# Unread products at the program borders, a reordered odd mixer and later rank products

## The reference

```python
x = x + (0.5 * (1.0 + mod[:, 2]) * f1).astype(x.dtype)
h = _adaln(x, w['norm_gain'][l, 1], mod, 1)
# even layer: gated DeltaNet heads | RWKV-7 heads;  odd layer: GLA heads | mLSTM heads
x = x + ((1.0 + mod[:, 5]) * o).astype(x.dtype)
```

```python
# C: qd = q*exp(bc); att = causal(qd @ (k*exp(-bc))); kd = k*exp(bc_last - bc)
#    o = att @ v + qd @ S;  S = S*exp(bc_last) + kd^T @ v
# D: dm = exp(log_d - m_t) * (q @ k^T); num = w_in*(q @ C) + dm @ v; den likewise
#    h = num / max(|den|, exp(-m_t)); then an RMS norm and a gate for both
```

```python
w_raw = w['w0_b'][i] + jnp.tanh(w_lr) @ w['w_w2'][i]
a = jax.nn.sigmoid(w['a0_b'][i] + a_lr @ w['w_a2'][i])
```

## Time and profile before

| | us |
|---|---|
| median of 3 runs | 2659.85 |
| the profiled execution | 2658.36 |
| its span, first to last instruction | 2656.6 |
| TensorE busy | 2541.6 |
| VectorE busy | 1604.7 |
| ScalarE busy | 1057.3 |
| POOL busy | 650.2 |

### The profile page before, as it was taken

How to read it: one execution, slowest core, us unless ns; L and a number is a source line. 1 busy time by engine, 2 the same in 40 slices (tenths; PEclk the granted TensorE clock), 3 DMA queues, 4 the chain that set the end, 5 groups by cost and what they waited for, 6 DMA issues and landing times. The chain is left out here.

```text
span 2656.6 us, 52472 instructions
## 1 busy us (share of the span) xinstructions
PE 2541.6 (96%) x22720; PEld 2389.8 (90%) x22720; DVE 1604.7 (60%) x2302; ACT 1057.3 (40%) x1546; POOL 650.2 (24%) x499
## 2 busy tenths in 40 slices
PE   6999999999999899999999999999999679999998
PEld 4999999888787787999999999999989569999998
DVE  5678726665465555677842677852743356677825
ACT  4444414554344322444432544432432333444513
POOL 0455201000010031155501055500100312355301
PEclk8999999999999979999999999999999789999999
DMA  6332455631000014222255322255751213222324
GB/s 238 104 120 95 157 192 193 236 131 54 29 3 3 9 60 163 64 95 93 93 194 177 121 90 96 96 183 175 234 200 60 76 52 105 66 94 96 101 83 133
DMA packets 82846, 303.30 MB, mean 114 GB/s; under 512 B 9376, under 2 KB 17072, under 8 KB 81336
## 3 DMA queue, kind: packets, MB, share of 16 engines
q1 hardware_dynamic: 82616, 299.95, 34.2%
HBM read 289.16 MB, written 10.76 MB: 113 GB/s over the span
## 5 line engine op out<-in xcount | busy, mean ns | idle before, releaser
L175 DVE TENSOR_TENSOR weights_r<-work,weights_r 128x1024 fp32r<-128x1024 f32 (+2 forms) x309 | 389.6, 1261 | 339.2 <-ACT weights_r L171 339.2
L171 ACT ACTIVATE weights_r<-work 128x1024 fp32r<-128x1024 f32 (+2 forms) x309 | 299.1, 968 | 534.0 <-PE banks L1498 298.9
L1379 POOL TENSOR_TENSOR rows<-rows,consts 128x288 f32<-128x288 f32 (+3 forms) x64 | 82.1, 1282 | 711.8 <-ACT consts L1641 711.8
L1496 PE MATMUL banks<-low_r,weights_r 128*128 128x288 f32 (+1 forms) x1064 | 255.3, 299 | 0.0
L1397 PE MATMUL banks<-big_r,weights_r 128*128 128x288 f32 x768 | 227.0, 296 | 0.0
L1398 PE MATMUL banks<-h_r,weights_r 128*128 128x288 f32 x768 | 226.6, 295 | 0.0
L1396 PE MATMUL banks<-h_r,weights_r 128*128 128x288 f32 x768 | 226.5, 295 | 0.0
L1494 PE MATMUL banks<-h_r,weights_r 128*128 128x288 f32 (+1 forms) x808 | 201.7, 307 | 4.7 <-DVE big_r L437 4.7
L1496 PE MATMUL banks<-big_r,weights_r 128*128 128x288 f32 (+2 forms) x800 | 202.0, 298 | 0.0
L175 DVE TENSOR_TENSOR ring_r<-consts,ring_r 128x1024 fp32r<-128x1024 f32 (+1 forms) x87 | 105.7, 1215 | 153.1 <-ACT ring_r L171 153.1
L1498 PE MATMUL banks<-h_r,weights_r 128*128 128x288 f32 (+1 forms) x808 | 195.3, 299 | 0.0
(11 more groups left out here) (581 smaller groups left out, 7084.9 us busy)
## 6 DMA issues: line engine op xcount, KB each, us to landing
work<-w_ff_dram SPq DMA_DIRECT2D x117, 512.0 KB, 3.6
h<-w_mod_dram SPq DMA_DIRECT2D x48, 768.0 KB, 5.3
consts<-w_ff_dram SPq DMA_DIRECT2D x59, 512.0 KB, 3.6
work<-w_down_dram SPq DMA_DIRECT2D x55, 512.0 KB, 3.5
big_buf<-w_mod_dram SPq DMA_DIRECT2D x24, 768.0 KB, 6.1
consts<-w_down_dram SPq DMA_DIRECT2D x33, 512.0 KB, 3.5
work<-w_down_dram SPq DMA_DIRECT2D x33, 384.0 KB, 3.4
work<-w_mod_first_dram SPq DMA_DIRECT2D x24, 512.0 KB, 12.0
```

The source lines that it names most:

```text
L171: return act.activation(high, raw, ACT.Copy)
L175: return engine.tensor_tensor(low, raw, high.bitcast(F32), ALU.subtract)
L1379: pool.tensor_tensor(k.rows[:, c], k.rows[:, c], k.square[:, c], ALU.add).then_inc(added, 1)
L1496: pe.matmul(out[a], high[:, w], x[a][1], start=False, stop=False)
```

## The change

1. `unread` issues products of two constant 128 x 128 matrices into a bank that nothing reads: 8 or 10 ahead of the first unit of each `dense_chain`; 10 at the end of the chain with the even projection (behind a wait for `unit7` of VectorE), 12 at the end of the one with the odd projection (behind `cols` of ScalarE); 8 in `even_prompt` ahead of `sq1_0` of chunk 0.
2. The rank product `r` goes from ahead of step 4 to ahead of step 6 of its piece (L1474).
3. In `odd_mixer`: the logs of the chunks are issued without waits, each with its semaphore. POOL masks the logs of chunk c between te and Kl of the same chunk, not one chunk ahead. TensorE does weights(0) ahead of front(1). ScalarE starts with Vc and Vd of chunk 0, and does Lexp and xw of i+2 right behind exponents(i+2), ahead of KL(i+1) and the root. VectorE does weights(1) behind front(1).

```diff
+def unread(k, pe, bank, count):
+    for _ in range(count):
+        pe.matmul(bank[:, 0:P], k.mask("ident"), k.mask("ones"), start=True, stop=True)
...
+                    if u is units[0]:
+                        unread(k, pe, banks(u, u.pieces[0])[:, 0], 8 if begin else 10)
...
-                            if even_gates and kt == KT // 2 and i in range(even_at(20), even_at(24)):
+                            if even_gates and kt == KT - 2 and i in range(even_at(20), even_at(24)):
                                 even_gates.rank(pe, "r", i - even_at(20))
...
+                if even_gates:
+                    pe.wait_ge(*even_gates.q.after("dve", "unit7"))
+                    unread(k, pe, k.psum[6], 10)
+                if odd_gates:
+                    pe.wait_ge(*odd_gates.q.after("act", "cols"))
+                    unread(k, pe, k.psum[6], 12)
...
+                        if c == 0 and g == G[0]:
+                            claim(f"sq1_{g}", c)
+                            unread(k, pe, two_banks(f"sq1_{g}", c)[0:P, 0], 8)
...
-        act += square_act(c) + of(i + 2, front_act) + of(i + 1, lambda b: at(b, ["KL"])) + at(c, ["root"]) \
-            + of(i + 2, weight_act)
+        act += square_act(c) + of(i + 2, front_act) + of(i + 2, log_act) + of(i + 1, lambda b: at(b, ["KL"])) \
+            + at(c, ["root"]) + of(i + 2, value_act)
...
-                    sp.wait_ge(logs_in, 16 * c)
                     chunk_logs(c)
...
-                pool.wait_ge(constants.landed, 32)
-                masked_logs(ODD_ORDER[0])
                 for i in places:
                     c = ODD_ORDER[i]
-                    if i + 1 < len(ODD_ORDER):
-                        masked_logs(ODD_ORDER[i + 1])
                     if c != SAMPLE:
                         relative(c, i)
                     to_the_end(c, i)
+                    masked_logs(c)
                     keys_to_end(c, i)
...
                 front(ODD_ORDER[0])
+                weights(ODD_ORDER[0])
                 front(ODD_ORDER[1])
-                weights(ODD_ORDER[0])
...
+                evict(ODD_ORDER[0], 0)
                 exponents(ODD_ORDER[0], 0)
-                evict(ODD_ORDER[0], 0)
+                log_exponents(ODD_ORDER[0], 0)
+                exponents(ODD_ORDER[1], 1)
+                keys(ODD_ORDER[0], 0)
+                log_exponents(ODD_ORDER[1], 1)
                 evict(ODD_ORDER[1], 1)
-                keys(ODD_ORDER[0], 0)
-                exponents(ODD_ORDER[1], 1)
```

More of the change, by code:

```diff
@@ L3409, in odd_orders @@
     front_act = lambda c: pick(c, "X Xn xl F", "X Xn xl")
-    weight_act = lambda c: at(c, ["Vc", "Vd"] + [f"Lexp_{h}" for h in range(2 if c == SAMPLE else 4)] + ["xw"])
+    log_act = lambda c: at(c, [f"Lexp_{h}" for h in range(2 if c == SAMPLE else 4)] + ["xw"])
+    value_act = lambda c: at(c, ["Vc", "Vd"])
     square_act = lambda c: pick(c, "sqC_0 sqC_1 sqD_0 sqD_1", "sqC sqD")
@@ L3419, in odd_orders @@
     of = lambda i, names: names(ODD_ORDER[i]) if i < len(ODD_ORDER) else []
-    masks_pool = lambda i: of(i, lambda c: at(c, ["lm"]))
-    pe = of(0, front_pe) + of(1, front_pe) + of(0, weight_pe)
-    act = of(0, front_act) + of(0, weight_act) + of(1, weight_act) + at(ODD_ORDER[0], ["KL"]) + of(1, front_act)
-    dve = of(0, front_dve) + of(0, weight_dve) + of(1, weight_dve) + of(0, masked_dve) + of(1, front_dve)
-    pool = masks_pool(0)
+    pe = of(0, front_pe) + of(0, weight_pe) + of(1, front_pe)
+    act = of(0, value_act) + of(0, front_act) + of(0, log_act) + of(1, front_act) + at(ODD_ORDER[0], ["KL"]) \
+        + of(1, log_act) + of(1, value_act)
+    dve = of(0, front_dve) + of(0, weight_dve) + of(0, masked_dve) + of(1, front_dve) + of(1, weight_dve)
+    pool = []
     for i in places:
         c = ODD_ORDER[i]
-        pool += masks_pool(i + 1)
         if c != SAMPLE:
@@ L3431, in odd_orders @@
         pe += of_sample(i + 1, "sc0 sc1") + (out_pe(SAMPLE) if of_sample(i + 1, "co") else [])
-        act += square_act(c) + of(i + 2, front_act) + of(i + 1, lambda b: at(b, ["KL"])) + at(c, ["root"]) \
-            + of(i + 2, weight_act)
+        act += square_act(c) + of(i + 2, front_act) + of(i + 2, log_act) + of(i + 1, lambda b: at(b, ["KL"])) \
+            + at(c, ["root"]) + of(i + 2, value_act)
         dve += sums_dve(c) + of(i + 1, masked_dve) + scaled_dve(c) + of(i + 2, front_dve) + of(i + 2, weight_dve)
         dve += of_sample(i, "SC2 SC3 SD2 SD3 SD4 SD5") + gated_dve(c) + of_sample(i + 1, "SC0 SC1 SD0 SD1")
-        pool += pick(c, "rel te Kl eC eD", "te Kl eC eD KEm KLm")
+        pool += pick(c, "rel te lm Kl eC eD", "te lm Kl eC eD KEm KLm")
     return pe, act, dve, pool
@@ L3492, in odd_mixer @@
         states_in, cleared, n_ready = (ph.sem(x) for x in ("states_in", "cleared", "n_ready"))
-        logs_in, sample_logs_in, entries_in = (ph.sem(x) for x in ("logs_in", "sample_logs_in", "entries_in"))
+        sample_logs_in, entries_in = (ph.sem(x) for x in ("sample_logs_in", "entries_in"))
+        logs_in = [ph.sem(f"logs_in_{c}") for c in range(NCH)]
         log_of = lambda c: log_rows[:, c * 4 * n:(c + 1) * 4 * n].rearrange("p (h i) -> p h i", h=4)
@@ L3513, in chunk_logs @@
                 def chunk_logs(c):
-                    sp.dma_start(log_of(c), log[None, :, c * n:(c + 1) * n].to_broadcast([P, 4, n])).then_inc(logs_in, 16)
+                    sp.dma_start(log_of(c), log[None, :, c * n:(c + 1) * n].to_broadcast([P, 4, n])).then_inc(logs_in[c], 16)
                 chunk_logs(0)
@@ L3601, in masked_logs @@
                         pool.wait_ge(sample_logs_in, 32)
+                        pool.wait_ge(constants.landed, 32)
                         tt(v2(log_rows_s), v2(log_rows_s), k.half("cut_below8")[:, None, :].to_broadcast([P, 2, m]), ALU.add)\
@@ L3604, in masked_logs @@
                         return
-                    pool.wait_ge(logs_in, 16 * (c + 1))
+                    pool.wait_ge(logs_in[c], 16)
+                    pool.wait_ge(constants.landed, 32)
                     tt(log_of(c), log_of(c), k.big("cut_below")[:, None, :].to_broadcast([P, 4, n]), ALU.add)\
@@ L3856, in evict @@
                 def evict(c, i):
-                    w = size(c)
                     act.wait_ge(*after("pe", "vct", c))
@@ L3864, in evict, with log_exponents @@
                         .then_inc(*did("Vd", c))
+                def log_exponents(c, i):
+                    w = size(c)
                     act.wait_ge(*after("pool", "lm", c))
@@ L3906, in _ @@
                         exponents(ODD_ORDER[i + 2], i + 2)
+                        log_exponents(ODD_ORDER[i + 2], i + 2)
                     if i + 1 < len(ODD_ORDER):
@@ L4066, in _ @@
                 weights(ODD_ORDER[0], 0)
-                weights(ODD_ORDER[1], 1)
                 masked(ODD_ORDER[0], 0)
                 front(ODD_ORDER[1], 1)
+                weights(ODD_ORDER[1], 1)
                 for i in places:
```

## The result

The changed kernel took 2634.66 us (median of 4 executions, 2631.5 to 2636.6) beside 2656.4 for the kernel before (4, 2651.05 to 2662.24): a ratio of 0.9921, 95% interval 0.9899 to 0.9943. A second comparison of the same two kernels gave 2639.76 against 2658.66, ratio 0.9931 (0.9910 to 0.9951). So 19 to 22 us were won by the medians (18 to 21 by the ratios), where 10.6 were forecast. The executions of one kernel lie up to 18 us apart here (26 of the kernel before: 2643.95 to 2661.5), so the intervals are some 0.2% to either side.

A forecast was written before the change was run, and what follows sets the result against it. TensorE was taken to set the end nearly everywhere, so only its waits or low clock pay. Terms -4.3 - 8.6 + 1.9 + 0.4 + 0 = -10.6 took 2658.36 to 2647.8, median 2649; range 2640 to 2657.

The forecast's parts named there:

- Later rank products: Even projection: TensorE's four waits of 1.07 us ahead of r vanish, gain 4.3 us.
- rival (c): Even projection: the rank wait only moves to the next w, total 2653 us; chance 0.08.
- Start of the odd mixer: Odd mixer's start: outputs of chunk 0 begin at 2095.2, 8.6 us earlier; ends 5.4 and 11.
- Everything starts about 0.75 us later: Odd mixer's start: the 12 unread products ahead of it delay everything by about 0.75 us.
- Steady rounds: Odd mixer's rounds: moved table load, Lexp and xw make round 1's root 1.9 us later; ends 0 and 5.7.
- The price of an unread product: Chain ends and borders: 0.11 us each at the odd border, 0.24 at half clock ahead of sq1_0.
- Round 0 still has the exponentials' table, and klt ends behind Lexp: nothing: Odd mixer, round 0: ScalarE's new order changes its time by nothing.
- a full clock gives at most some tenths: Ahead of the two output projections: first unit bound by VectorE's splits, so unread products gain only tenths; term 0.
- rival (d): Odd mixer's samples' part falls to half clock, at most 16 us more, 2665 us; chance 0.09.
- (b): Odd mixer: start gives only 5.4 through late logs, or ScalarE binds three rounds; 2653 us; chance 0.19.
- Rival (a): Clock kept over borders: -2.1 for +0.4 in the even mixer, -2 at the start; 2644.5 us; chance 0.12.
- rival (e): Everywhere: unread products don't hold the clock; already in the sum, no separate chance.

The follow-up runs named there:

- e2: Kernel before with only the reordered odd mixer, no unread products or later ranks: 2647.99 us, ratio 0.9960.
- j1: h3 plus 12 unread products in every odd mixer round, between the two groups' transposes: 2630.84 us, ratio 0.9907 to the kernel before.
- i1: Kernel before, old order, plus 22 unread products ahead of the odd mixer's first key transposes and 7 behind its second front: 2653.47 us, ratio 0.9978.
- e4: Changed kernel without its unread products (later ranks and reordered odd mixer kept): 2639.12 us, ratio 0.9941 to the kernel before.
- h2: Kernel before, old order, plus 20 unread products behind the odd mixer's first front, queued behind the waiting key transposes: 2660.95 us, ratio 1.0007.
- e3: Kernel before with only the six groups of unread products added: 2656.81 us, ratio 1.0003.
- h3: Changed kernel with ScalarE's old steady order, unread products only at dense 2 and 3 (10 each) and the odd start's wait (24): 2634.03 us, 0.9921 to before.

## Why the prediction was wrong

The direction was right, and the terms for the ranks, the start and the steady rounds were near. The size was half, since the sum had no term for the clock of untouched work.

- **Later rank products**, forecast -4.3: -4.6 in every trace with them. The wait did not move to the next `w`, rival (c) is out.
- **Start of the odd mixer**, forecast -8.6: -7.9 up to the first outputs in this pair of profiles, -6.1 against the second profile of before, and -7.2 between the averages (four profiles with the old start and nothing added there, two of the changed kernel). It is near, with a wrong part in it. "Everything starts about 0.75 us later" was 2.0: the next program's first work came 2.0 us behind the last projection product before (2078.45) and 4.0 after (2068.18). Only 1.0 of that reached the outputs: in e2, without the unread products, they come 18.5 us behind that product, not 19.5.
- **Steady rounds**, forecast +1.9: +1.4 to +2.3, 1.6 on average, around the root of round 1 in the nine profiles with ScalarE's new order, and 0.0 to +0.8, 0.4 on average, in the eight others (j1 aside). So the order costs some 1.2: the right mechanism, the size somewhat less.
- **The price of an unread product** was mis-sized. I took 0.11 us, from four transposes in 0.60. But a transpose is one instruction and a product of two such matrices is two: 24 instructions in 2.84 us, so 0.24 at full clock, and 4.05 for ten where the first 3.3 us go at half clock. All 58 are 116 instructions, and keep TensorE busy for 20.0 us in the changed kernel.
- **The step that failed** is the rounds and borders themselves: "Round 0 still has the exponentials' table, and klt ends behind Lexp: nothing", and for the dense starts "a full clock gives at most some tenths". I counted waits and orders, and priced all products of the odd mixer at the clock of the trace of before. With the earlier start TensorE waits less ahead of the outputs: they and the weights behind them run at full clock, -4.6 to -6.4 over the rest of round 0 in all twelve profiles with the new start, against -0.8 to +0.1 in the five others with the old one and its waits. e2 shows that the order alone does it, i1 that filled waits do it with the old order. At the start of dense 2 the chain's first dozen pairs went at 0.48 us apiece and now go at 0.265, some 2 us; at dense 3 it is 1. Together that is 8 us of the 8 to 11 that the forecast lacked.
- **The even tail** is no part of the gain. Its -7.9 in the profiled execution is one of the lengths that stretch has in any of these kernels; the second profile of the changed kernel has -1.6 there and the same span to 1 us.
- **The samples' part** stayed at 1.00 in both profiles of the changed kernel, so rival (d) is out for it. Its mechanism is there on a small scale: eight of the 19 profiles, e2 and e4 among them, have 3.4 us of half clock at the beginning of that part, and it costs 1.2 us in e2. POOL's logs came in time (2074.03), so (b) is out.
- **Rival (a)** was the true one in kind, at the wrong places. At the even mixer's start the products do shorten the half clock: it is 6.8 us long in all eight profiles that have them there and 10.2 or 13.7 in the eleven others. But no time came of it (the steps over the even mixer are +1.5 and -0.8), while at the dense starts it did. And rival (e), that the products don't hold the clock anywhere, was in the sum at 0.11 us apiece, half of their price or less; what they would cost with no clock returned, no run here shows.

Not settled: the parts alone (0.9996, 0.9960 and 1.0003) multiply to 0.9959, the whole is 0.9921 and 0.9931. The 7 to 10 us between them are about as large as the intervals taken together; I can't say whether the parts help each other (what follows an earlier end with a higher clock would) or it is spread.

## What to carry to other kernels

Price every product behind a wait at both clocks, and ask of each removed or shortened wait what the engine will run at afterwards: here a start some 7 us shorter brought 5 us more through the clock of the work behind it. Products that nobody reads paid where they filled a wait that was already there, ahead of dense work, on a bank that was free then. Put behind the waiting instruction in the queue they only delayed (h2), in a round without that wait they cost 2.45 us for twelve (j1), and all of the border products together cost what they gave (e3). Don't count a higher mean clock as time won before the steps show it. And compare steps between two profiles only beside a second profile of the same kernel: one stretch that nobody had touched moved by 6 us on its own.

## What the runs showed of the hardware

The granted clock has two levels here, 1.00 and 0.50. In h3 the stretch from 2096 to 2115, with a wait of 3.06 us in it and TensorE busy for 15.05 of 19.00 us, has a mean of 0.68; in j1 the same work with that wait filled has 1.00. The Trainium skill (TensorE: Matmul & The Clock Gate, Loop structure matters more than you think) says that VectorE's copies beside the products do no harm to the clock and that a long wait inside the loop does; its example is a wait of 8 us for DMA. The trace agrees in kind, with a shorter wait, and for VectorE.

The clock also fell where TensorE was not idle: in the even tail it goes down near 956, behind products of 16 columns that begin at 951.23, and TensorE counts as busy for 9.00 of 9.00 us at 0.50 (the ends of products are modelled in these rows). I had not expected that of a full queue, and no run here varies those products, so the cause stays open. How long it stays down varied between executions of one kernel, from 13.7 to 27.3 us. The Trainium skill (TensorE: Matmul & The Clock Gate, What's actually happening) says that the point at which the clock rises varies from run to run by some 0.5 us either way, with where the first product falls in the gate's own timing. That the point varies, the runs agree; by how much, they don't: 13.6 us here.

The mean clock of an execution tells its time, within one kernel: 2.1 us for 0.001. A mean lower by 0.001 over 2656 us is 5.3 us more at half clock (2656 x 0.001 / 0.5), so a microsecond at half clock cost 0.4 us of time, near the 0.5 that work without a gap would lose. Between kernels with and without unread products it did not hold: e3 has 0.0037 more clock than the kernel before and the same time.
